# LRU gate blocks in two groups of four behind the two panels of q1, and the last conv ahead of the rope, in a two-layer hybrid encoder trunk

## The reference

```python
xn = rmsnorm(x, pre_mix_g[l])
proj = xn @ w_in[l]          # -> u_lru | g_lru | q | k | v | gate_a | gate_b
# branch A, the RG-LRU
uc = conv_b + sum(upad[:, k:k + S] * conv_w[k] for k in range(4))     # causal, depthwise
ub = uc.reshape(B, S, 16, 64)                                         # 16 blocks of 64 channels
r = sigmoid(einsum("bsnd,nde->bsne", ub, w_a) + b_a)
i = sigmoid(einsum("bsnd,nde->bsne", ub, w_x) + b_x)
log_a = -8.0 * r * softplus(-lam)
a = exp(log_a)
b = sqrt(-expm1(2.0 * log_a)) * i * uc
h = associative_scan(a, b)
y_a = (h * gelu(g_lru)) @ w_pa[l]
# branch B: rotary on q and k, sliding-window attention with sinks
y_b = swa_sink_attention(q, k, v, cos, sin, sinks) @ w_pb[l]
mixed = (sigmoid(gA) * y_a + sigmoid(gB) * y_b) @ w_o[l]
x = x + rmsnorm(mixed, post_mix_g[l])
x = x + rmsnorm((silu(h2 @ w_ffn_gate) * (h2 @ w_ffn_up)) @ w_ffn_down, post_ffn_g[l])   # h2 = rmsnorm(x)
```

## Time and profile before

| | |
|---|---|
| Median of three timed runs | 818.22 us (817.62 to 818.77) |
| The profiled execution | 817.47 us, span 815.7 us |
| Mean granted clock of TensorE | 0.995 of full speed |
| PE busy | 800.0 us (98%) |
| DVE busy | 601.6 us (74%) |
| ACT busy | 461.2 us (57%) |
| DMA | 156.48 MB, mean 192 GB/s |

### The profile page before, as it was taken

One profiled execution on the slowest core, in us unless ns is written; L12 is line 12 of the kernel. 1 busy time (PEld: TensorE's weight loads), 2 busy tenths in 40 slices (PEclk: granted clock), 3 DMA queues, 4 the chain that ended last, 5 costly groups with the idle time before them and its releaser, 6 DMA issues.

```text
span 815.7 us, 10533 instructions
## 1 busy us (share of the span) xinstructions
PE 800.0 (98%) x4250; PEld 670.9 (82%) x4250; DVE 601.6 (74%) x601; ACT 461.2 (57%) x591; POOL 79.1 (10%) x136
## 2 busy tenths in 40 slices
PE   8999999999998999999999999999999989999997
PEld 6897898888886888888889889988888868888885
DVE  5799897557669778667489869964658796985762
ACT  6467967644454655545355787764426555565441
POOL 2841000000220000000011200000004000000000
PEclk9999999999999999999999999999999999999999
DMA  9776453545477697863476745434645588778501
GB/s 292 254 247 203 149 176 106 162 148 207 142 271 221 190 314 204 237 227 104 155 215 226 257 138 172 155 117 148 242 165 169 175 250 266 221 234 258 197 9 53
DMA packets 84274, 156.48 MB, mean 192 GB/s; under 512 B 7313, under 2 KB 27905, under 8 KB 84226
## 3 DMA queue, kind: packets, MB, share of 16 engines
q1 hardware_dynamic: 80000, 147.42, 53.2%
q0 software_dynamic: 4224, 8.39, 6.1%
q10 hardware_dynamic: 2, 0.00, 0.0%
HBM read 154.75 MB, written 1.05 MB: 191 GB/s over the span
## 4 chain that ended last, share of the span: by engine, by line
PE 92%; DVE 5%; ACT 1%; issue 0%; POOL 0%; DMA 0%; DVEq 0%; POOLq 0%; ACTq 0%
PE work L768 13%; PE work L770 12%; PE work L769 12%; PE acc L768 9%; PE acc L770 9%; PE acc L769 9%; PE work L760 4%; PE work L761 4%; PE work L762 4%; PE work L854 3%; PE work L855 3%; PE work L856 3%; DVE weights_lo L1527 2%; PE work L954 1%; PE acc L879 1%; PE work L902 1%
## 5 line engine op out<-in xcount | busy, mean ns | idle before, releaser
L1527 DVE TENSOR_TENSOR weights_lo<-weights_raw,weights_hi 128x2048 fp32r<-128x2048 f32 x114 | 260.3, 2289 | 96.6 <-ACT weights_hi L1140 96.4
L1140 ACT ACTIVATE weights_hi<-weights_raw 128x2048 fp32r<-128x2048 f32 x116 | 221.8, 1916 | 157.9 <-PE work L770 79.7
L768 PE MATMUL work<-weights_hi,act_a_hi 128*128 128x512 f32 x416 | 165.6, 398 | 0.0
L770 PE MATMUL work<-weights_hi,act_a_lo 128*128 128x512 f32 x416 | 163.5, 393 | 0.0
L769 PE MATMUL work<-weights_lo,act_a_hi 128*128 128x512 f32 x416 | 163.3, 392 | 0.0
L768 PE MATMUL acc<-weights_hi,act_b_hi 128*128 128x512 f32 x240 | 94.8, 395 | 0.0
L770 PE MATMUL acc<-weights_hi,act_b_lo 128*128 128x512 f32 x240 | 93.7, 390 | 0.0
L769 PE MATMUL acc<-weights_lo,act_b_hi 128*128 128x512 f32 x240 | 93.4, 389 | 0.0
L768 PEld LDWEIGHTS work<-weights_hi,act_a_hi 128*128 128x128 f32 x416 | 78.8, 190 | 17.2 <-issue 0.8
L770 PEld LDWEIGHTS work<-weights_hi,act_a_lo 128*128 128x128 f32 x416 | 78.8, 189 | 16.9
L769 PEld LDWEIGHTS work<-weights_lo,act_a_hi 128*128 128x128 f32 x416 | 79.0, 190 | 15.8
(11 more groups left out here) (216 smaller groups left out, 1268.3 us busy)
## 6 DMA issues: line engine op xcount, KB each, us to landing
weights_raw<-in_w_in SPq DMA_DIRECT2D x43, 1024.0 KB, 5.2
weights_raw<-in_w_ffn_gate SPq DMA_DIRECT2D x16, 1024.0 KB, 7.5
weights_raw<-in_w_ffn_up SPq DMA_DIRECT2D x12, 1024.0 KB, 6.1
weights_raw<-in_w_ffn_down SPq DMA_DIRECT2D x12, 1024.0 KB, 5.0
weights_raw<-in_w_pa SPq DMA_DIRECT2D x8, 1024.0 KB, 5.1
weights_raw<-in_w_pb SPq DMA_DIRECT2D x8, 1024.0 KB, 5.0
weights_raw<-in_w_o SPq DMA_DIRECT2D x8, 1024.0 KB, 4.9
q_feat<-in_w_ffn_down SPq DMA_DIRECT2D x6, 1024.0 KB, 8.8
```

Source lines behind the costliest of these rows:

```text
L768: mm(dst, xh, wh, start=first, stop=False)
L770: return mm(dst, xl, wh, start=False, stop=final)
L1140: activate(w_hi[:, SLOT[n], :], raw_slot(RAWS[n]), ACT.Copy).then_inc(hi_done.sem, 1)
L1527: v.tensor_tensor(w_lo[:, SLOT[n], :], raw_slot(RAWS[n]), bits(w_hi[:, SLOT[n], :]), ALU.subtract).then_inc(split_done.sem, 1)
```

## The change

In PE's list u0 to u3 now follow one another without gates between them. The gates come in two groups of two pairs: columns 0 to 3 behind q1's first panel, columns 4 to 7 behind its second. ACT drains them at the same two places. The list of PSUM uses follows: u in banks 0 to 3, then gates 0 to 3, gates 4 to 7 and gate_a, each in banks 0 to 3. In layer 0 DVE makes rope (q0, 1) behind conv(3) in place of conv(2). Nothing else is changed, and the number of instructions is the same on each engine.

```diff
-    uses = four("xn") + [("u", 0), ("u", 1), ("u", 2), ("gates", 0), ("gates", 1), ("u", 3)]
-    uses += [("gates", 2), ("gates", 3)] + [("gates", c) for c in range(4, 8)] + four("gate_a")
+    uses = four("xn") + four("u") + [("gates", c) for c in range(8)] + four("gate_a")
...
-                f_product("u", 0, xn_hi, xn_lo)
-                f_product("u", 1, xn_hi, xn_lo)
-                pe.wait_ge(*gate_w_loaded.at(l, 64))
-                for j in range(2, 4):
+                for j in range(4):
                     f_product("u", j, xn_hi, xn_lo)
-                    gates(2 * j - 4, 2 * j - 2)
-
                 pe.wait_ge(*rope_read.at(l, 3 if first else 2))
                 for j in range(2):
                     t_product("q1", j, [acc[:, 0, :], acc[:, 1, :]], xn_hi, xn_lo)
-                    gates(4 + 2 * j, 6 + 2 * j)
+                    if j == 0:
+                        pe.wait_ge(*gate_w_loaded.at(l, 64))
+                    gates(4 * j, 4 * j + 4)
...
-                    if name == "u" and j > 1:
-                        gates(2 * j - 4, 2 * j - 2)
                     if (name, j) == ("q1", 0):
-                        gates(4, 6)
+                        gates(0, 4)
                     if (name, j) == ("q1", 1):
-                        gates(6, 8)
+                        gates(4, 8)
                         decay(0)
...
-                    if first and name == "u" and j < 3:
-                        rope(*ROPES[1 + j])
+                    if first and name == "u" and j != 2:
+                        rope(*ROPES[min(1 + j, 3)])
```

## The result

The changed kernel takes 831.63 us (median of 6 runs, 831.12 to 832.46) against 817.99 us (median of 6, 817.55 to 818.88): ratio 1.0172, 95% interval 1.0162 to 1.0182, so 13.6 us slower. The prediction was 831.1 us, 826.5 to 834.5. The profiled execution of after, at 832.46 us, is the longest of the six; its span is 830.7 us, 15.0 more than that of before.

A forecast was written before the change was run, and what follows sets the result against it. PE, busy 98% of the span, was taken as the bound. Losses 5.7 (layer 0), 3.2 (layer 1), 3.2 and 0.8 (clock) sum to 12.9 us on 817.47, giving 830.4; predicted median 831.1, range 826.5 to 834.5.

The forecast's parts named there:

- The bounds: Whole kernel: PE is busy 98% of the span, so its stalls are paid in full; ACT or DVE count where PE waits.
- The gain of a merge: Gates on PE: a two-pair group costs 1.98 us, against 1.22 per single pair; 0.92 us saved a layer, 1.84 in all.
- Layer 0, q1: q1's first panel: still starts at 60.99, held by DVE's rope; PE stands still 2.6 us, removing two pairs gains nothing.
- Layers 0 and 1, gate_a: gate_a's first matmul waits for ACT's third-pair drain: stall of 3.55 us each layer; 5.7 us lost in layer 0, 3.2 in layer 1.
- The table load: Sigmoid table load in ACT's chain before the drains: 1.29 us by the row, without the skill page's extra 1.38 us drain.
- The clock: PE's clock falls behind new stalls: 1.6 us at gate_a in each layer, 0.8 at q1 (middle of nothing and 1.6).
- the clock does not fall: Rival, behind the new stalls: they occur but the clock stays up, 827.1 us; no fall or one has chance 0.12.
- Given back: Rival, feed-forward part: PE's two waits for DVE (6.2 us, plus 3.2 slow clock) shrink, 822 to 826 us; chance 0.08.
- The other side: Rival, gate_a's bank claim: third pair already drained, no cost there; 816.4 or 818.8 us; chance 0.03 gain, 0.02 no change.

The follow-up runs named there:

- experiment 4: Changed kernel with idle transposes for PE in its three stalls (20 ahead of q1 in layer 0, 27 ahead of gate_a per layer): 826.48 us.
- experiment 6: Kernel before with only the first two gate pairs merged, behind u3: 816.85 us; with rope (q0, 0) ahead of (kv, 1) too: 816.94; that rope order alone: 817.1.
- experiment 1: Kernel before with only layer 0's rope (q0, 1) moved behind conv(3): 817.35 us; changed kernel with that rope back behind conv(2): 831.57 us.
- Experiment 2: Changed kernel with layer 0's ropes in layer 1's order, (q0, 0) ahead of (kv, 1): 827.38 us.
- Experiment 3: Changed kernel with ACT draining the third pair of gates before the split behind q1's second panel, both layers: 825.43 us.
- experiment 5: Changed kernel with a one-column sigmoid on ACT behind u3's split, so its table is loaded there: 827.93 us.
- experiment 8: 24 idle transposes meant for PE's feed-forward wait: on the kernel before 821.08 us; on one merge (first two pairs, behind u3) plus early rope (q0, 0) 822.84.
- experiment 7: Changed kernel with rope (q0, 0) early in layer 0, sigmoid table loaded behind u3's split, third pair drained before the second split: 822.29 us.

## Why the prediction was right

**The bounds.** PE's new stalls are paid in full: the waits, less the merges, make up 9.05 us in experiment 4 against 8.9 predicted.

**The gain of a merge.** 0.46 us each was predicted; 0.4 is what one gives in experiment 6. By the prediction's own reckoning a group of 32 costs 2.09 us in the changed kernel (70.66 - 68.11 = 2.55 from the last matmul ahead to the second behind, less 0.46), against 1.98.

**Layer 0, q1.** "q1 still starts at 60.99": it started at 61.27, and PE stood still for 2.58 us against 2.6. The start is held by the ropes, as said. The length of the wait agrees so closely by some luck, since it moves with PE's own start: 3.7 us in experiment 1 where PE came 1.2 us earlier. Experiment 2 shows that this is a loss in series.

**Layers 0 and 1, gate_a.** The waits are 3.51 us twice, against 3.55. ACT's chain took 81.97 - 68.53 = 13.44 us against 13.23; of the 0.2 us, 0.11 lie between the first split and the table load and 0.11 in the first two drains. Experiment 3 shows the split in the chain, experiment 5 the table load.

**The table load.** The row decided rightly: 1.28 us of load and the next sigmoid 0.01 us behind it in the changed kernel too, and experiment 5 moved ACT's drains by 1.4 us, not by 2.7. The further 1.38 us that the Trainium skill gives for each switch ("ScalarE: Activation LUTs", "What ACT_TABLE_LOAD costs") shows in no run here.

**The clock.** This was the term with the least certainty: 3.2 + 0.8 = 4.0 us predicted, 5.1 measured in experiment 4 and 1.49 + 1.3 + 2.4 = 5.2 in the profile. In the profiled execution the fall behind the 2.6 us wait, taken at a half, came in full (1.49), and behind gate_a in layer 1 the clock was low for longer than the 3.2 us of the earlier trace rows (2.4 lost and not 1.6); in layer 0 gate_a lost 1.3. So the profiled execution misses its own forecast by 2.1 us (832.46 against 830.4), and the median, 831.63 against 831.1, by 0.5. The close hit of the median is in part luck: the price of a fall is an average over falls that differ from one execution to the next, and one of the three was an even bet.

The price itself was read at a place where it is not paid. "Half of 3.2 us, 1.6, is lost; the second wait does the same" is true of PE's matmuls, but the kernel loses only about 0.2 us of it there, as the profiles in experiment 8 show. At q1 and gate_a no second wait stands behind the stall, so there it is paid: 5.1 us for three falls in experiment 4, 1.7 each.

**Of the rivals,** "the clock does not fall" fails at the three windows. "Given back" fails: the two waits in the feed-forward part are 3.1 us as before, and their slow clock had next to nothing to give. The other side failed at gate_a's claim, and experiment 7 shows that with the chain as short as I could make it PE still waits 2.1 us there.

## What to carry to other kernels

Before merging small groups of matmuls, ask what each of them stood in front of: here they covered a wait for another engine at one place, and at the other gave the drain of a PSUM bank a whole panel's time. A merge saved 0.4 us of PE here; a bank that is claimed by a near neighbour costs the whole queue of the draining engine, which includes whatever it does first (here a split of 1.8 us). And price a new stall of PE at its length and, where it is over 2 us, at half as much again, since the clock may fall behind it: 5.1 us on top of 9.05 in experiment 4. That holds where PE is the bound behind the stall. Before you try to win a slow clock back, look at what PE would wait for next.

## What the runs showed of the hardware

The fall of TensorE's clock behind a stall is not a fixed price. In the profiles, waits of 3.5 us at gate_a had a fall each time (six cases, in the changed kernel and experiments 1 and 2), and waits of 1.7 us none in two cases. Between them it varied: of two waits of 2.1 us in experiment 7 one had a fall, and two of 2.8 us in experiment 5 had one each; a wait of 2.6 us had one in the changed kernel and none in experiment 5. Behind the 3.1 us waits in the feed-forward part the clock fell both times in the kernel before, but it stayed up once each in experiments 2, 5 and 7. Experiment 7's windows around that wait:

```profile
655.00:659.00 4.00, 1.63 (x10) 1.14 (x8) 4.00 (x3) 1.86 (x1) 0.00 (x0) 1.00 1.04 417
659.00:663.00 4.00, 3.27 (x17) 2.79 (x18) 4.00 (x3) 2.94 (x4) 1.33 (x1) 1.00 1.02 280
```

How long the clock stays low varied too, from some 3 us to more than 6 (experiment 3, 60 to 66 us). Each fall at q1 or gate_a cost 1.3 to 2.4 us in the changed kernel's profile, which is the likely reason for the wider spread of the kernels with such stalls.

What a fall costs the kernel depends on what stands behind it: 1.3 to 2.4 us where PE is the bound, about 0.2 us in the feed-forward part, where DVE is.
